# Expert weights fetched ahead of the expert stage, and the order in which seats and weighted copies are made

## The reference, cut to what matters

```python
for i in range(DEPTH):                       # 2 layers
    ...
    h = x * (1.0 + scale) + shift
    y = stick_breaking_attention(...) if i % 2 == 0 else retention(...)
    x = layer_norm_2(ALPHA * x + (1.0 + gate) * y, ...)
    ...
    y = grouped_moe(h, router_w, router_b, w_gate[i], w_up[i], w_down[i])
    x = layer_norm_2(ALPHA * x + (1.0 + gate) * y, ...)

def grouped_moe(...):
    logits = t @ router_w + router_b         # 16 experts in groups of 4
    ...                                      # best group, its two best experts, two weights a token
    for e in range(N_EXPERTS):
        hidden = silu(t @ w_gate[e]) * (t @ w_up[e])          # 1024 -> 512
        out = out + combine[:, e:e+1] * (hidden @ w_down[e])  # 512 -> 1024
```

## Time and profile before

| | |
|---|---|
| median of three runs | 2118.43 us (2115.28 to 2121.6) |
| the profiled execution | 2120.26 us, its span 2118.5 us |
| HBM read | 440.25 MB, 208 GB/s over the span |
| attention, 1100 to 1230 us | TensorE busy, few transfers |
| first MoE stage | about 1230 to 1508 us |
| retention | about 1508 to 1816 us |
| second MoE stage | about 1816 us to the end |
| transfers in 1300 to 1400 us | 427 GB/s |

### The profile page before, as it was taken

How to read it: one execution, slowest core, us unless ns; L and a number is a source line. 1 busy time by engine, 2 the same in 40 slices (tenths; PEclk the granted TensorE clock), 3 DMA queues, 4 the chain that set the end, 5 groups by cost and what they waited for, 6 DMA issues and landing times. The chain is left out here.

```text
span 2118.5 us, 24179 instructions
## 1 busy us (share of the span) xinstructions
PE 1851.4 (87%) x9830; PEld 1294.2 (61%) x9830; DVE 788.0 (37%) x1629; ACT 549.3 (26%) x983; POOL 229.3 (11%) x217
## 2 busy tenths in 40 slices
PE   7987898899989777899999869999789989599995
PEld 7676875599887443798886544444578564344432
DVE  1263543467530452566411252221340041522223
ACT  1124223266420222566312421111111020211111
POOL 0000000333120030443020120000100000200000
PEclk9898998999999777899999979999899999799998
DMA  7322176354434561444524079999434312689992
GB/s 273 119 80 80 40 277 240 139 183 176 178 139 160 233 283 40 179 160 160 219 104 155 6 286 392 427 428 427 180 139 150 141 67 80 278 345 427 427 427 120
DMA packets 33557, 442.94 MB, mean 209 GB/s; under 512 B 3868, under 2 KB 4128, under 8 KB 6944
## 3 DMA queue, kind: packets, MB, share of 16 engines
q1 hardware_dynamic: 29520, 426.78, 50.7%
q0 software_dynamic: 2480, 8.92, 1.2%
q10 hardware_dynamic: 1440, 5.61, 0.7%
HBM read 440.25 MB, written 1.05 MB: 208 GB/s over the span
## 5 line engine op out<-in xcount | busy, mean ns | idle before, releaser
L82 PE MATMUL ps<-xTs,ring 128*128 128x256 f32 (+1 forms) x1856 | 366.8, 359 | 12.8 <-ACT xTs L88 12.8
L82 PE MATMUL ps<-ring,arena 128*64 128x512 f32 (+1 forms) x992 | 340.2, 608 | 21.7 <-DVE arena L99 9.0
L82 PEld LDWEIGHTS ps<-xTs,ring 128*128 128x128 f32 x1856 | 323.2, 199 | 52.5 <-issue 17.4
L88 ACT ACTIVATE arena<-ps 128x384 f32<-128x384 f32 (+5 forms) x229 | 99.0, 433 | 764.8 <-PE ps L82 580.9
L82 PE MATMUL ps<-xsplit_f,wsplit_f 128*128 128x256 f32 x2112 | 260.3, 286 | 16.8 <-DVE xsplit_f L91 12.3
L82 PEld LDWEIGHTS ps<-xsplit_f,wsplit_f 128*128 128x128 f32 x2112 | 258.1, 195 | 19.4 <-DVE xsplit_f L91 13.1
L82 PE MATMUL ps<-ringx,arena 128*64 128x512 f32 x960 | 257.7, 602 | 10.2 <-DMA ringx<-in_mu 5.2
L82 PEld LDWEIGHTS ps<-ring,arena 128*64 128x64 f32 (+1 forms) x992 | 124.2, 158 | 223.8 <-issue 205.1
L91 DVE TENSOR_TENSOR wsplit_f<-ring,wsplit_f 128x1024 fp32r<-128x1024 f32 x132 | 163.0, 1242 | 50.7 <-ACT wsplit_f L88 50.7
L82 PE MATMUL ps<-arena 128*128 128x128 f32 (+5 forms) x1128 | 152.7, 321 | 25.0 <-DVE arena L91 23.7
L82 PEld LDWEIGHTS ps<-arena 128*128 128x128 f32 (+2 forms) x1128 | 135.8, 203 | 41.2 <-DVE arena L91 24.6
(11 more groups left out here) (143 smaller groups left out, 1567.3 us busy)
## 6 DMA issues: line engine op xcount, KB each, us to landing
ring<-in_ada SPq DMA_DIRECT2D x24, 2048.0 KB, 8.5
ring<-in_wu SPq DMA_DIRECT2D x22, 2048.0 KB, 7.9
ringx<-in_mu SPq DMA_DIRECT2D x20, 2048.0 KB, 23.7
ringx<-in_md SPq DMA_DIRECT2D x20, 2048.0 KB, 25.3
ringx<-in_mg SPq DMA_DIRECT2D x20, 2048.0 KB, 26.0
ring<-in_mg SPq DMA_DIRECT2D x14, 2048.0 KB, 19.8
ring<-in_mu SPq DMA_DIRECT2D x14, 2048.0 KB, 22.8
ring<-in_md SPq DMA_DIRECT2D x14, 2048.0 KB, 25.6
```

Of the source, the lines that this page charges most:

```text
L82: return self.e.matmul(o, l, r, start=start, stop=stop, skip_group_check=True)
L88: return self.e.activation(o, i, f, **k)
```

## The change

It has three parts.

1. The order of loads and the slots. The first three blocks of the first MoE stage go ahead of attention's two output weights, the first two of the second ahead of retention's four. Slots are given anew: in each round of eight the first five blocks go to the five slots of `ringx` in the order of `EXTRA`, the last three to `ring`, whose turn goes on. Slots in `ABOVE` lie above the memory of the stage before, so they no longer wait for that stage: in the first MoE stage they wait for the end of ffn(1) (`"pre", 3`), in the second for the use of their former block. The others wait for VectorE's last copy of attention's outputs (`"sbo", 15`) or for retention's last normalised output (`"rout", 7`).
2. The memory of attention, retention and MoE is laid out for that: what is read last lies lowest, `ringx` comes last in MoE, the arenas shrink, and the decay table goes into the place of the masks among the constants (1024 KB, still loaded by ACT's queue). A gate row's copy in retention shares its place with later temporaries.
3. `seats(i)` makes all `pm` first, then all `pw`; `way_back` waits for the `pw` of its group. The gather and POOL's `rows_applied` wait for `pm`, as before, which is now counted before the copies.

```diff
--- before.py
+++ after.py
@@ -196,32 +196,34 @@
     out += ffn(0)
     out += [("wo", j) for j in range(4)]
     out += [("wov", 0), ("wov", 1)] + [("ada", 2 + k // 6, k % 6) for k in range(12)] + [("woo", 0), ("woo", 1)] + ffn(1)
-    out += [("ws", j) for j in range(6)] + [("wso", 0), ("wso", 1)]
-    out += moe_loads(0, 0, 12)
-    out += [("wr", j) for j in range(8)] + [("wrv", j) for j in range(4)]
-    out += [("wro", j) for j in range(4)]
-    out += moe_loads(1, 0, 12)
+    one, two = moe_loads(0, 0, 12), moe_loads(1, 0, 12)
+    out += [("ws", j) for j in range(6)] + one[:3] + [("wso", 0), ("wso", 1)] + one[3:]
+    out += [("wr", j) for j in range(8)] + [("wrv", j) for j in range(4)] + two[:2] + [("wro", j) for j in range(4)] + two[2:]
     return out
 LOADS = all_loads()
+EXTRA = [(5, 6, 7, 3, 4), (6, 7, 3, 4, 5)]
+ABOVE = [(5, 6, 7), (6, 7)]
 def all_slots():
-    out, used, last, turn, base, was = {}, {}, {}, 0, 0, None
+    out, used, last, turn, seen = {}, {}, {}, 0, [0, 0]
     for name in LOADS:
         if name[0] in ("mg", "mu", "md"):
-            if was != name[1]:
-                was, base, turn = name[1], turn, 0
-            k = turn % WIDE
-            i = (base + k) % SLOTS if k < SLOTS else k
+            k = seen[name[1]] % WIDE
+            seen[name[1]] += 1
+            i = EXTRA[name[1]][k] if k < WIDE - SLOTS else (turn + k - WIDE + SLOTS) % SLOTS
         else:
-            if was is not None:
-                was, turn = None, base
             i = turn % SLOTS
-        turn += 1
+            turn += 1
         used[i] = used.get(i, 0) + 1
         out[name] = (i, used[i], last.get(i))
         last[i] = name
@@ -475,11 +477,12 @@
         O.qd, O.kdT, O.kdt, O.Sg = (rows(m.take(256), 2, 128) for _ in range(4))
     with ExitStack() as st:
-        m = Arena(st, 4, 17000)
-        B.qk = rows(m.take(4096), 16, 256)
-        B.vs = m.take(2048).rearrange("p (t n) -> p t n", t=2)
+        m = Arena(st, 4, 5014 + 2 * 4096)
         B.oT = rows(m.take(2048), 8, 256)
         B.gk = m.take(1024)
+        B.vs = m.take(2048).rearrange("p (t n) -> p t n", t=2)
+        B.qk = rows(m.take(4096), 16, 256)
         B.az = [m.take(384) for _ in range(5)]
         B.sp = [m.take(384) for _ in range(5)]
@@ -487,7 +490,6 @@
         with ExitStack() as st:
             m = Arena(st, 5 + 2 * l, 3470)
             M[l].eids = st.enter_context(nc.sbuf_tensor(f"eids{l}", [128, 8], I32))
-            M[l].ringx = st.enter_context(nc.sbuf_tensor(f"ringx{l}", [128, (WIDE - SLOTS) * 4096], F32))
             M[l].qs, M[l].rk, M[l].co, M[l].col = (m.take(n) for n in (96, 32, 48, 42))
             M[l].spt, M[l].rem = m.take(96), m.take(16)
             M[l].xg = rows(m.take(2048), 8, 256)
@@ -499,18 +501,20 @@
             M[l].yl, M[l].pt = ylo, [way[:, i, :] for i in range(2)]
             M[l].pu = xTs[:, 1536:2048]
             M[l].pw = M[l].pu.rearrange("p (t n) -> p t n", t=2)
+            M[l].ringx = st.enter_context(nc.sbuf_tensor(f"ringx{l}", [128, (WIDE - SLOTS) * 4096], F32))
             M[l].xh, M[l].xl = ([ap[:, h, :] for h in range(2)] for ap in (xhi, xlo))
     with ExitStack() as st:
-        m = Arena(st, 6, 24800)
+        m = Arena(st, 6, 5014 + 3 * 4096)
+        Q.gT = rows(m.take(4096), 16, 256)
         Q.qk = rows(m.take(4096), 16, 256)
-        Q.gT = rows(m.take(4096), 16, 256)
         Q.vr = m.take(4096).rearrange("p (t n) -> p t n", t=2)
-        Q.dec = m.take(2048)
+        Q.dec = kc[:, masks:masks + 2048]
         Q.cs = m.take(512)
         Q.tmpr = [m.take(512) for _ in range(3)]
-        Q.gk = m.take(1024)
         Q.rtmp = [m.take(384) for _ in range(3)]
+        Q.gk = m.ap[:, m.top:m.top + 1024]
         Q.otmp = [m.take(512) for _ in range(3)]
     DM = kc[:, kat["dm0"][0]:kat["dm0"][0] + 768].rearrange("p (g n) -> p g n", g=3)
@@ -1050,6 +1054,7 @@
             def way_back(q):
                 o = 128 * GROUP[q][1]
+                t.wait_ge(*v("pw", n, GROUP[q][0]))
                 b = bank("ptT", n, q, ring=MOE_BANKS)
                 for h in range(2):
                     tr(b[:, 128 * h:128 * h + 128], m.pm[:, h, o:o + 128].bitcast(F32))
@@ -1780,15 +1785,15 @@
                 if first_q:
                     v.wait_ge(*t("hT" if first_q == ALONE + 1 else "ptT", n, first_q - 1))
                 v.own()
-                for j, pair in enumerate(GROUPS[i]):
-                    for e in range(2):
-                        p, o = PAIR[pair][e % len(PAIR[pair])], 128 * j + 64 * e
-                        for h in range(2):
-                            chosen, rank, weight = where(l, p, h)
-                            v.tensor_scalar(m.pm[:, h, o:o + 64], K("iota")[:, 0:64], rank, chosen, ALU.is_equal, ALU.mult) \
-                                .then_inc(s_dve, v.did())
-                            v.tensor_scalar(m.pw[:, h, o:o + 64], K("iota")[:, 0:64], rank, weight, ALU.is_equal, ALU.mult) \
-                                .then_inc(s_dve, v.did("pm", n, i))
+                for weighted in (False, True):
+                    for j, pair in enumerate(GROUPS[i]):
+                        for e in range(2):
+                            p, o = PAIR[pair][e % len(PAIR[pair])], 128 * j + 64 * e
+                            for h in range(2):
+                                chosen, rank, weight = where(l, p, h)
+                                dst, by, key = (m.pw, weight, "pw") if weighted else (m.pm, chosen, "pm")
+                                v.tensor_scalar(dst[:, h, o:o + 64], K("iota")[:, 0:64], rank, by, ALU.is_equal, ALU.mult) \
+                                    .then_inc(s_dve, v.did(key, n, i))
             def again(j):
@@ -2549,10 +2554,14 @@
                 dst = ring[:, i * 4096:i * 4096 + width(name)]
             else:
                 dst = M[name[1]].ringx[:, (i - SLOTS) * 4096:(i - SLOTS) * 4096 + 4096]
-            if i >= SLOTS and (old is None or old[1] != name[1]):
+            if i >= SLOTS and (old is None or old[1] != name[1]) and i not in ABOVE[name[1]]:
+                s.wait_ge(*(v("rout", 7) if name[1] else v("sbo", 15)))
+            elif i >= SLOTS and old is None:
                 for lane in (t, v, a, g):
-                    s.wait_ge(*lane("pre", 4 + 2 * name[1]))
+                    s.wait_ge(*lane("pre", 3))
             elif old is not None:
                 s.wait_ge(*(t("used", old) if ("used", old) in t.at else v("used", old)))
             s.dma_start(dst, src).then_inc(s_ring[i], 16)
```

## The result

| | median | executions |
|---|---|---|
| before | 2119.44 us | 7 (2115.28 to 2122.15) |
| changed | 2127.56 us | 7 (2123.8 to 2131.72) |

The ratio is 1.0039, 95% interval 1.0024 to 1.0054: the change costs 8.1 us, and the interval leaves no change out. The forecast was 2122, +3.6, with a range of 2112 to 2129. The profiled execution of the changed kernel took 2124.59 us (span 2122.9), the one of the kernel before 2120.26 (2118.5).

The account below looks back on a forecast made before the run. The prediction took T, followed by a fixed 213 us of full weight transfers, to bound each MoE stage. 0 for the early loads and +3.6 for the seats' order on 2118.4 gave 2122 us, range 2112 to 2129.

Parts of the forecast that it names:

- The bound: MoE stages: 43 blocks of transfers, 213 us, follow T, so a stage ends a fixed time after T.
- T: First weight-block issue after all eight slots filled, when the first pair's gate product is done: 1274.57 and 1864.77 us.
- Part 1 worth nothing: Weight loads ahead of the MoE stages: fetching first blocks earlier gains 0, ends -1 and +1 us.
- The gather 1.8 us earlier: Start of each MoE stage: gather waits for 8 operations, not 16; T 1.8 us earlier twice, -3.6 us.
- POOL released into VectorE's copies: Ahead of T: POOL's four row operations and VectorE's weighted copies exclude each other, delaying scalings and gate copy.
- How many copies pass: Gaps between POOL's operations: one or two copies; corners -0.1, +1.8, +5.5 and +7.4, middle +3.6 us.
- the corner of one a gap: One copy between POOL operations: gate copy ends 13.7 us after gather's start; +3.9 and +1.6, together +5.5 us.
- The clock: First stage, gate copy's end to T: if TensorE idles as in the second, 11.9 us, 1.9 more.
- the upper corner: Ahead of T: one copy a gap in both stages plus the first stage's clock price, +7.4 us.
- (a): VectorE's queue: the train of copies keeps POOL out until it is through; -2.7 us, 2115.7; chance 0.23.
- (b): VectorE's queue before the first scaling: one copy a gap, first expert at half clock; +7.4 to +10.4, 2127.5; chance 0.22.
- (c): Gather on TensorE: its earlier start brings the clock up at its beginning; -8.0 us, 2110.4; chance 0.08.

Follow-up runs that it names:

- e3: Changed kernel with POOL's row operations of a MoE stage waiting for VectorE's gate copy instead of the first seats: 2117.25 us, ratio 0.9992.
- e2: Changed kernel with seats and copies made in turn again, leaving early loads, new slots and new layout alone: 2119.40 us, ratio 1.0002.
- e6: Kernel before with the seats' new order, POOL's row operations and row loads made late, no early weight loads: 2111.93 us, ratio 0.9958.
- e5: Changed kernel with POOL's row operations waiting for the gate copy and its row loads issued after the weight blocks landed: 2112.36 us, ratio 0.9961.
- e8: Changed kernel with the first group's eight weighted copies made by ScalarE instead of VectorE: 2112.40 us, ratio 0.9965.
- e1: Kernel before with only the seats' new order (all seats, then all weighted copies): 2127.70 us, ratio 1.0044.
- e4: Changed kernel with POOL's row operations waiting for the first group's weighted copies: 2116.44 us, ratio 0.9988.
- e7: Changed kernel with each of POOL's four row operations of a MoE stage cut into two of 512 columns: 2121.74 us, ratio 1.0013.

## Why the prediction was right and where not

1. **The bound.** Right. T decides, and from T to the last landing 214.7 to 215.2 us pass in every version but e3 (213 by the prediction's sum of 43 blocks).
2. **Part 1 worth nothing.** Right, shown by e2 and again by e6.
3. **The gather 1.8 us earlier, -3.6 us if alone.** Right in size: it starts 25.16 us after the norm's first transposition instead of 26.96. But -3.6 is not what the new order is worth alone: with no weighted copy locked out, e5, e6 and e8 gained 7.3 to 7.8, since the second stage's gate copy and its clock, and a faster gather (7c), come on top.
4. **POOL released into VectorE's copies, which take turns.** Right, and it is the cause of the loss: e1 has it alone and loses 8.6, e4 and e8 take it away and are faster than before, e7 shortens each turn and leaves +2.0. The copies that were held up take 2.35 to 2.55 us, POOL's operations 2.3 to 2.5. The trace agrees with the Trainium skill, SBUF — State Buffer, Who interferes with whom, that a VectorE operation in a two-port mode and a GpSimd operation exclude each other for a whole instruction; that the copies run in such a mode is not seen in a trace.
5. **How many copies pass.** This is the term that was mis-sized. I took the middle of four corners, +3.6, as if a mixture of gaps with one and with two copies would end half way. It does not: all six waiting copies are done before POOL's fourth operation only if two pass in every one of the three gaps. In the three executions of the change and in e1, 17 of 24 gaps let one through and 7 let two, and the copies always ended behind the fourth, as in the corner of one a gap. There I had the gate copy's end at 13.7 us; measured were 13.3 and 14.5, so with the 1.8 gained +3.5 and +2.4, together +5.9 where that corner had +5.5. The 14.5 has a link that I did not see, the gather waiting for a bank that a small copy behind the weighted ones empties.
6. **The clock.** In the first stage its price came nearly as feared: from the gate copy's end to T 11.6 us (1267.84 to 1279.42) instead of 10.0; I had taken 11.9, the second stage's. In the second it fell from 11.9 to 10.8, which I had left as it was. So the clock ahead of T cost +0.4 in sum, not the +1.9 of the upper corner, and T is 6.2 us later in sum (5.0 and 1.2). The other 2 us or so of the measured +8.1 lie behind T and in retention; they were in no term, and their cause is open.
7. **The rivals.** (a), a train that keeps POOL out, is wrong: POOL got in after the second copy. (b) named the right place and the right way of passing, and its argument, POOL's next operation dispatched 0.08 us after the last, was the one row that spoke on the question; I gave it 0.22 and should have given it more. That +8.1 lies in its +7.4 to +10.4 is in part luck, since ahead of T only 6.2 came about, and the first expert, which it had at half clock, ran at 1.00 (window 1272.30 to 1279.40). (c) is partly right in its mechanism and wrong in its size. The gather's first 2.7 us ran at the slow rate (0.43 us from one product to the next) in the first stage and 4.0 in the second, against 4.9 and 5.7 before: the clock did rise sooner. Its last product started 5.1 to 5.2 us after its first instead of 6.0 in the first stage, which is 0.8 us, not 2.2. In the changed kernel this was lost in the idle time that followed; in e5, e6 and e8 it came through, where T of the first stage is 1.9 to 2.6 us earlier, in e8 after 0.7 us of waiting for POOL.

The forecast of +3.6 had the right sign and less than half of the size. The upper corner alone gives 2125.8; the range held 2127.56 because it reached on into rival (b).

## What to carry to other kernels

When a step is split so that its first half can be signalled earlier, list everybody who waits for that signal, not only the one you want to start. Here the second waiter, POOL, locked VectorE out of the second half, and TensorE, which was to gain, came to T 5.0 us later in the first stage. And before loads are moved forward ask what the consumer waited for: with the same number of slots, all full before the first is used, earlier fetching bought nothing (e2, e6). What is moved off the critical path takes its transfers with it: in e3 1.05 MB of row loads that landed in a stretch bound by transfers cost 3.3 and 2.9 us there; before, they fell into idle time. And where two outcomes alternate at random, ask what a mixture of them does before taking the middle.

## What the runs showed of the hardware that I had not expected

- Between two POOL operations on the same half of x, which follow each other by 0.08 us, one or two of a train of VectorE operations 0.22 us apart get through (9 gaps of 16 with one, 7 with two, in the change's three executions and e1). Between POOL's second and third, on different halves, where the trace has the next starting 0.04 us before the last ends, it was one in all 8. The copy behind the one that was held up is dispatched 0.1 us before POOL's next operation in the first kind of gap, and together with it in the second. In e7 it is one of 1.3 us a gap, now and then two.
- ScalarE's copies beside POOL's operations took 2.02 us for eight, VectorE's 10.46: ScalarE was not held up by POOL in this case.
- A copy of 0.7 us that waits for the end of an operation already running lost 0.1 to 1.9 us; a train of eight short ones lost 8.6 (10.46 instead of the 1.88 of e3).
